# A two-layer decoder trunk: other orders in the embedding gate, at the layer boundary and in the last norm, and one more filler ahead of the gather

## The reference

```python
for i in range(2):
    x = x + mixer_block(rms_norm(x, ln_mix_g[i]), ...)            # projections, conv, attention, conv module
    x = x + hier_moe(rms_norm(x, ln_ffn_g[i]), ...)               # top-2 of 32 experts
    h = rms_norm(x, ln_ple_g[i])
    x = x + sigmoid(h @ w_ple_gate[i]) * (p[i] @ w_ple[i])        # the embedding gate
return rms_norm(x, final_norm_g)
```

## Time and profile before

| | before |
|---|---|
| time, median of 3 runs | 1158.5 us (1156.49 to 1158.56) |
| the profiled execution: time | 1154.8 us |
| the profiled execution: span from first to last instruction | 1153.0 us |
| PE busy | 95% of the span |
| DVE busy | 56% |
| ACT busy | 31% |
| mean granted TensorE clock | 0.989 of 2.4 GHz |

### The profile page before, as it was taken

The page is one execution under the profiler, slowest core; times in us unless marked ns, Lnnn a source line. Parts: engine busy times, 40 slices in busy tenths (PEclk is TensorE's granted clock), DMA queues, the critical chain, the costliest instruction groups (busy, mean ns, idle before and its releaser), DMA issues.

```text
span 1153.0 us, 21335 instructions
## 1 busy us (share of the span) xinstructions
PE 1091.3 (95%) x8152; PEld 858.7 (74%) x8152; DVE 650.3 (56%) x1353; ACT 354.4 (31%) x598; POOL 134.8 (12%) x163
## 2 busy tenths in 40 slices
PE   5999999999899999998899999999999999999985
PEld 5988998998755555554889799999886555555564
DVE  6687997545533333334768789964546333333365
ACT  4345442234321111112554454323333111111142
POOL 0121320110001001000002032101100100100000
PEclk9999999999999999999989999999999999999997
DMA  7557975555289999998454777555644999999951
GB/s 207 136 159 243 311 230 145 154 159 165 110 339 418 416 417 419 419 417 305 129 147 127 248 255 237 172 160 146 184 170 173 397 416 417 418 418 419 413 162 44
DMA packets 202981, 300.39 MB, mean 261 GB/s; under 512 B 14000, under 2 KB 166544, under 8 KB 186512
## 3 DMA queue, kind: packets, MB, share of 16 engines
q1 hardware_dynamic: 202896, 299.28, 73.3%
HBM read 298.21 MB, written 1.05 MB: 260 GB/s over the span
## 4 chain that ended last, share of the span: by engine, by line
PE 74%; DVE 12%; DMA 5%; issue 5%; ACT 2%; POOL 1%; SPq 1%; DVEq 0%; POOLq 0%; ACTq 0%
PE ps L729 72%; DMA gu_ring<-in_w_exp_up_dram 4%; DVE wsplit L1810 3%; PE ps L732 2%; DVE work L1932 1%; ACT wsplit L1276 1%; DVE work L1760 1%; DMA ring<-in_w_in_dram 1%; DMA ring<-in_w_o_dram 0%; DVE h_pair L2135 0%; DMA work<-in_x_dram 0%; DVE work L1880 0%; DVE work L1834 0%; DVE h_pair L1819 0%; DVE work L1904 0%
## 5 line engine op out<-in xcount | busy, mean ns | idle before, releaser
L729 PE MATMUL ps<-h_pair,wsplit 128*128 128x256 f32 x2880 | 369.8, 288 | 14.6 <-DVE h_pair L1819 7.4
L729 PEld LDWEIGHTS ps<-h_pair,wsplit 128*128 128x128 f32 x2880 | 356.1, 194 | 22.8 <-issue 14.8
L1810 DVE TENSOR_TENSOR wsplit<-ring,wsplit 128x1024 fp32r<-128x1024 f32 x136 | 167.4, 1235 | 71.7 <-ACT wsplit L1276 68.5
L1276 ACT ACTIVATE wsplit<-ring 128x1024 fp32r<-128x1024 f32 x136 | 141.6, 1055 | 198.2 <-PE ps L729 110.3
L729 PE MATMUL ps<-gu_ring,hT 128*64 128x256 f32 x896 | 107.6, 383 | 2.0 <-DMA gu_ring<-in_w_exp_up_dram 1.8
L1932 DVE SCALAR_TENSOR_TENSOR work<-work,convT 128x256 f32<-128x256 f32 x240 | 104.7, 508 | 0.0
L1503 ACT ACTIVATE prow<-ps 128x128 f32<-128x128 f32 x64 | 17.7, 277 | 277.0 <-PE ps L729 277.0
L2222 DVE TENSOR_TENSOR hT_r<-ps,hT_r 128x512 fp32r<-128x512 f32 x64 | 44.3, 692 | 93.6 <-ACT hT_r L1276 93.6
L729 PEld LDWEIGHTS ps<-gu_ring,hT 128*64 128x64 f32 x896 | 61.7, 137 | 46.6 <-issue 13.3
L2208 DVE TENSOR_TENSOR prow<-prow,ps 128x128 f32<-128x128 f32 x64 | 18.4, 288 | 131.6 <-ACT prow L1503 131.6
L729 PE MATMUL ps<-work,ring 128*128 128x256 f32 x384 | 85.7, 379 | 0.0
(11 more groups left out here) (211 smaller groups left out, 1139.5 us busy)
## 6 DMA issues: line engine op xcount, KB each, us to landing
ring<-in_w_in_dram SPq DMA_DIRECT2D x104, 512.0 KB, 4.7
down_ring<-in_w_exp_down_dram SPq DMA_DIRECT2D x40, 1024.0 KB, 19.1
gu_ring<-in_w_exp_gate_dram SPq DMA_DIRECT2D x28, 1024.0 KB, 14.7
gu_ring<-in_w_exp_up_dram SPq DMA_DIRECT2D x28, 1024.0 KB, 16.9
lent_down<-in_w_exp_down_dram SPq DMA_DIRECT2D x24, 1024.0 KB, 19.5
gu_last<-in_w_exp_gate_dram SPq DMA_DIRECT2D x12, 1024.0 KB, 13.9
gu_last<-in_w_exp_up_dram SPq DMA_DIRECT2D x12, 1024.0 KB, 16.1
ring<-in_w_exp_gate_dram SPq DMA_DIRECT2D x12, 1024.0 KB, 14.7
```

Of the source, the lines that this page charges most:

```text
L729: return nc.tensor.matmul(o, lhsT, rhs, start=first, stop=last)
L1276: return nc.scalar.activation(o, i, ACT.Copy)
L1810: TT(tile_split[:, m, 1, :, :], tile_of(name, m), tile_split[:, m, 0, :, :].bitcast(F32), ALU.subtract).then_inc(tile_low, 1)
```

## The change

It changes the order of instructions at four places, adds a filler in each layer, and computes the last norm in another way.

- `project_open`: the products of a kind are put together. First all of chunks 0 to 5 (high by high for both halves, then high by low for both, then low by high for both), then all three kinds of chunks 6 and 7 for m = 0, then for m = 1.
- `keep_busy` ahead of the gather runs 2 fillers instead of 1.
- `open_gate`: ACT squares all four pairs before it rounds the tiles of pg1. DVE makes two of the additions of squares ahead of the first low tile of pg1, and the others between the two.
- The gate and the boundary: ACT rounds the first tile of pg3 before the sigmoids and the second right after two of them; DVE takes pg2 before the first product, finishes three pairs of `xT`, splits all three, and takes pg3 only after that (in layer 1, which has no next layer, there is no split).
- The last norm: DVE multiplies the tokens in PSUM by the gain first, into the new `x_gain`, while the sum of squares is under way. PE's sum goes over four tiles (0 and 1, which hold pairs 0 to 2 added, and 6 and 7) instead of one, so two additions of squares are left out. The norm is then applied to `x_gain` by DVE for the first half of each row block and by ACT for the second.

```diff
@@ end of SP's program
-                    sp.wait_ge(pmul_ready[DEPTH], 2 * t + half + 1)
+                    sp.wait_ge(act_scaled if half else pmul_ready[DEPTH], t + 1)
@@ PE, project_open
-                    for chunks in (range(DC - 2), range(DC - 2, DC)):
-                        for m in range(2):
-                            rounded_rows(m, chunks)
-                        for m in range(2):
-                            rest_of_rows(m, chunks)
-                            rest_of_weights(m, chunks)
+                    early, late = range(DC - 2), range(DC - 2, DC)
+                    for m in range(2):
+                        rounded_rows(m, early)
+                    for m in range(2):
+                        rest_of_rows(m, early)
+                    for m in range(2):
+                        rest_of_weights(m, early)
+                    for m in range(2):
+                        rounded_rows(m, late)
+                        rest_of_rows(m, late)
+                        rest_of_weights(m, late)
@@ PE, ahead of the gather
-                keep_busy(UI["pp2"] % BANKS, 1)
+                keep_busy(UI["pp2"] % BANKS, 2)
@@ PE, end_of_all
-                    stat("mix", [sq_x[:, 0, :]], [(sq_added[l], all_added("mix"))])
+                    stat("mix", [sq_x[:, c, :] for c in (0, 1, 6, 7)], [(sq_added[l], 2), None, (sq_ready[l], 4), None])
@@ ACT, open_gate
-                    square_pair(0)
-                    square_pair(1)
-                    high_tile(l, "pg1", 0)
-                    square_pair(2)
-                    square_pair(3)
-                    high_tile(l, "pg1", 1)
+                    for i in range(4):
+                        square_pair(i)
+                    high_tiles(l, "pg1")
@@ ACT, gate and boundary
                 high_tiles(l, "pg2")
+                high_tile(l, "pg3", 0)
                 ple_sigmoid(0)
                 ple_sigmoid(1)
-                high_tile(l, "pg3", 0)
-                next_high(0)
                 high_tile(l, "pg3", 1)
                 ple_sigmoid(2)
-                next_high(1)
                 if l + 1 < DEPTH:
+                    next_high(0)
                     high_tile(l + 1, "kv", 0)
-                next_square(0)
-                next_high(2)
-                if l + 1 < DEPTH:
+                    next_high(1)
                     high_tile(l + 1, "kv", 1)
-                ple_sigmoid(3)
-                next_square(1)
-                next_square(2)
-                next_high(3)
-                next_square(3)
+                    next_high(2)
+                    ple_sigmoid(3)
+                    for i in range(3):
+                        next_square(i)
+                    next_high(3)
+                    next_square(3)
+                else:
+                    for i in range(2):
+                        act.wait_ge(x_gated, 4 * l + i + 1)
+                        next_square(i)
+                    ple_sigmoid(3)
+                    for i in (2, 3):
+                        act.wait_ge(x_gated, 4 * l + i + 1)
+                        next_square(i)
+
+            act.wait_ge(pow_ready[DEPTH], 1)
+            for t in range(TC):
+                act.wait_ge(gain_applied, TC + t + 1)
+                nc.scalar.activation(xout[:, t, 512:D], x_gain[:, t, 512:D], ACT.Copy, scale=col[:, 0, 1, t:t + 1]).then_inc(act_scaled, 1)
@@ DVE, open_gate
                     low_tile(l, "pg0", 1)
+                    add_square_pair(l, "ple", sq_p, 1)
+                    add_square_pair(l, "ple", sq_p, 2)
                     low_tile(l, "pg1", 0)
-                    add_squares("ple", sq_p, 4)
+                    add_square_pair(l, "ple", sq_p, 3)
+                    add_last_squares(l, "ple", sq_p, 4)
                     low_tile(l, "pg1", 1)
@@ DVE, gate and boundary
                 low_tile(l, "pg3", 0)
+                take("pg2", two(ple_t[2]))
                 ple_mul(0)
                 add_gated(0)
-                take("pg2", two(ple_t[2]))
                 low_tile(l, "pg3", 1)
                 ple_mul(1)
                 add_gated(1)
+                ple_mul(2)
+                add_gated(2)
+                dve.wait_ge(x_gated, 4 * l + 1)
                 if goes_on:
                     dve.wait_ge(vec_ready, 2 * (l + 1) + 2)
                     next_low(0)
-                ple_mul(2)
-                add_gated(2)
-                if goes_on:
                     next_low(1)
+                    next_low(2)
                     low_tile(l + 1, "kv", 0)
-                dve.wait_ge(x_gated, 4 * l + 1)
-                take("pg3", two(ple_t[0]))
-                if goes_on:
-                    next_low(2)
-                else:
-                    add_square_pair(l + 1, "mix", sq_x, 1)
-                    add_square_pair(l + 1, "mix", sq_x, 2)
-                ple_mul(3)
-                add_gated(3)
-                if goes_on:
+                    take("pg3", two(ple_t[0]))
                     low_tile(l + 1, "kv", 1)
+                    ple_mul(3)
+                    add_gated(3)
                     next_low(3)
                     add_square_pair(l + 1, "mix", sq_x, 1)
                 else:
-                    add_square_pair(l + 1, "mix", sq_x, 3)
-                    add_last_squares(l + 1, "mix", sq_x, 4)
+                    take("pg3", two(ple_t[0]))
+                    add_square_pair(l + 1, "mix", sq_x, 1)
+                    ple_mul(3)
+                    add_gated(3)
+                    add_square_pair(l + 1, "mix", sq_x, 2)
@@ DVE, last norm
+            dve.wait_ge(init_loaded, 48)
+            for half in range(2):
+                for t in range(TC):
+                    dve.wait_ge(tok_psum[l], 2 * half + 2)
+                    at = slice(half * 512, (half + 1) * 512)
+                    TT(x_gain[:, t, at], ps[:, 4 + 2 * t + half, :], gfull[:, at], ALU.mult).then_inc(gain_applied, 1)
             mean("mix", D)
             dve.wait_ge(pow_ready[l], 1)
-            dve.wait_ge(init_loaded, 48)
-            dve.wait_ge(tok_psum[l], 4)
+            dve.wait_ge(x_gated, 4 * DEPTH)
             for t in range(TC):
-                for half in range(2):
-                    STT(xout[:, t, half * 512:(half + 1) * 512], ps[:, 4 + 2 * t + half, :], col[:, 0, 1, t:t + 1],
-                        gfull[:, half * 512:(half + 1) * 512], ALU.mult, ALU.mult).then_inc(pmul_ready[l], 1)
+                dve.wait_ge(gain_applied, t + 1)
+                TS(xout[:, t, 0:512], x_gain[:, t, 0:512], col[:, 0, 1, t:t + 1], None, ALU.mult).then_inc(pmul_ready[l], 1)
```

More of the change, by code:

```diff
@@ L322, in program @@
         xout = area(9216, TC, D)
+        x_gain = area(0, TC, D)
         ang = area(8192, 4, S)
@@ L454, in program @@
         x_gated = sem("x_gated")
+        gain_applied = sem("gain_applied")
+        act_scaled = sem("act_scaled")
         psig_ready = sem("psig_ready")
@@ L1558, in next_high @@
                     act.wait_ge(x_gated, 4 * l + i + 1)
-                    if l + 1 < DEPTH:
-                        for c in (2 * i, 2 * i + 1):
-                            last = nc.scalar.activation(h_high[:, c, :], xT[:, c, :], ACT.Copy, scale=vcol("mix", c))
-                        last.then_inc(rows_high[l + 1], 1)
+                    for c in (2 * i, 2 * i + 1):
+                        last = nc.scalar.activation(h_high[:, c, :], xT[:, c, :], ACT.Copy, scale=vcol("mix", c))
+                    last.then_inc(rows_high[l + 1], 1)
                 def next_square(i):
```

## The result

| | kernel before | changed kernel |
|---|---|---|
| median (range), us | 1157.49 (1154.75 to 1158.56), 4 runs | 1143.07 (1141.55 to 1145.49), 4 runs |
| the profiled execution, us | 1154.8 | 1145.49 |
| its span, us | 1153.0 | 1143.7 |
| mean granted clock | 0.989 | 0.994 |

A forecast was written before the change was run, and what follows sets the result against it. PE was taken as busy 95% of the span, its gaps in the changed stretches set by ACT and DVE steps. Gains 0.65 + 0.45 + 2.9 + 1.4 + 3.85 = 9.25 us gave 1158.5 - 9.3 = 1149.2 us, range 1145.5 to 1153.7.

The forecast's parts named there:

- the term for the filler: Gather of layer 0: a second filler shortens the gap and keeps the clock up, 1.4 us; layer 1 counted 0.
- Openings: Where the gates open: PE no longer idles before the sum of squares; gain 0.65 us in layer 0, 0.45 in layer 1.
- The cover by pg0: Openings: ACT's four squares run while PE multiplies pg0; without that cover they would cost 1.1 us on the path.
- Boundary: Layer 0 to layer 1: earlier tiles and `xT` pairs bring 4.25 us, less 1.35 for a clock fall: 2.9 us.
- The charge for one fall of the clock: Boundary: new gaps bring one low stretch of about 3.3 us, 15 matmuls instead of 26, costing 1.35 us.
- 0.4 us as the worst: Gather of layer 1: the second filler counts 0, at worst a loss of 0.4 us, as the gap there is short.
- End, to the power: Last norm: POOL's power starts 4.3 us earlier, 0.45 of it from the opening, so the end's term is 3.85 us.
- The clock rival: Clock falls at gather (+1.4), boundary (+1.4) and last sum (+1.5) add 4.3 us: 1153.5 us; chance 0.20.
- the likeliest case: Whole kernel: the forecast itself, within 2.5 us of 1149.2 us, last sum taken at full clock; chance 0.62.
- The change doesn't do what it says: PE's work is the bound, expert loads absorb upstream gains, about half the end remains: 1156.5 to 1158.5 us; chance 0.07.
- slower: New boundary gaps keep TensorE at 1.2 GHz into layer 1; about 32 us low gives 1161 us; chance 0.04.
- The boundary gives nothing: Splits ahead of pg3's take put ACT and DVE in series, losing the boundary's 2.9 us: 1152.1 us; chance 0.07.

The follow-up runs named there:

- b1: Kernel before with only the new order in `open_gate`, both layers; ratio 1.0001, median 1155.95 us.
- c2: Changed kernel with one filler ahead of the gather instead of two; ratio 0.9930, median 1146.71 us.
- b3: Kernel before with only the second filler ahead of the gather added; ratio 1.0000, median 1155.83 us.
- b4: Kernel before with only the new gate order of layer 1 and the new last norm; ratio 0.9966, median 1151.58 us.
- e2: Changed kernel plus one filler in PE's wait for the last pair of `xT` at the boundary; ratio 0.9909, median 1144.46 us.
- d4: Changed kernel with the old last norm but the new gate order of layer 1; ratio 0.9918, median 1146.83 us.
- b2: Kernel before with only the new gate order of layer 0 and the new `project_open`; ratio 0.9982, median 1154.12 us.
- e4: Changed kernel with no filler ahead of the gather; ratio 0.9930, median 1146.03 us.
- c1: Changed kernel itself, run again in a second comparison with the kernel before; ratio 0.9929, median 1147.34 us.
- e1: Changed kernel itself, run a fourth time against the kernel before; ratio 0.9924, median 1146.57 us.
- c3: Changed kernel with the gate of layer 0 and `project_open` in the old order; ratio 0.9943, median 1148.01 us.
- d2: Changed kernel with PE's opening of layer 0 moved ahead of the end of the branch; ratio 0.9947, median 1149.73 us.

## Why the prediction was right or wrong

**Which step failed.** The forecast missed at the low end of its range, 1143.07 us for 1145.5 to 1153.7. The step that failed is the last of its sum, 1158.5 - 9.3 = 1149.2: it took the median of three runs for the time of the kernel before. The mean of 72 runs is 1155.7 us, so the base was 2.8 us too high. By the means of all runs the change gives 9.8 us (1155.7 to 1145.95 in 22 runs), so the gain was 0.5 us too small. The remaining 2.9 us are the spread of the four runs of the changed kernel, whose median lies that much under the mean of the 22. Within the gain the term for the filler was too large, the stores and PE's start behind the branch were put at nothing and measured 1.5 us won and 1.4 us lost, and these errors largely cancelled. Part by part:

**Openings: right.** No idle time before the sums, gains of 0.77 and 0.62 us to the sum for 0.65 and 0.45. The cover by pg0 held. In layer 0 PE starts later than before, so the stretch from its first matmul says less there; but from the filler to the sum b1 and c2, in which it starts early, take 12.12 us where before, b3 and b4 take 12.66 to 12.91.

**Boundary: mechanism right, size of the fall too large.** Without a fall the step gave 4.25 us, so 26.90 - 4.25 = 22.65; the profiles at full clock show 22.77. The charge for one fall of the clock was 1.35 us, and it cost 0.5 to 0.8 (23.23 to 23.59 against 22.77), although nearly as many matmuls ran slowly as I had put there. The 34 matmuls from 581.97 took 5.61 us, where e2 at full clock takes 1.45 + 3.10 = 4.55 for them. But e2 waits 0.34 us for ACT's tile between the two groups, and PE at the low clock reaches it when it is ready. From the start of the 34 to the sum the difference is 5.44 - 4.97 = 0.47 us. The term left that wait out. Against the old order the step is smaller, though: before had its own fall, of twice the length, and the old order takes 25.2 us at full clock. The order is worth 2.5 us; the other 1.2 of the 3.65 is the difference of two falls. Over all profiles the new order averages 23.4 us in 11 and the old one 25.7 in 5, falls counted in, so 2.3 us. The fall stayed in 9 of 11 executions. The Trainium skill ("TensorE: Matmul & The Clock Gate", section "HAM oscillation — how this bites in real kernels") describes a kernel whose clock falls behind each long wait for data. The trace differs in this: here the fall came behind four waits for ACT and DVE, the longest of 1.4 us.

**Filler: mechanism right, worth too large.** Its term, 1.4 us, was the difference between the gathers of two layers in one execution. That is what a fall costs (1.43 us in the rows), not how often it comes: it needed the share of executions in which the clock would fall within this gather, 2 of 5 with one filler. The mechanism held: in no profile with two fillers did the clock fall there. The "0.4 us as the worst" is seen as a begin 0.46 us late in either layer, but it doesn't reach the first expert. Measured: 0.0 us with 1.3 on either side (b3), and about 0.9 us by the rows and the counts.

**End, to the power: right in size, wrong in its cause.** 4.24 us for 3.85. The forecast had the last pair of `xT` 3.4 us earlier and gave 0.4 us to the new sum and the products ahead of the power. Measured are 4.19 us at the last pair and 0.05 behind it, and d4 shows the old norm as fast to the power. So two errors partly cancel. The products do end last, as forecast (1134.65 + 2.48 = 1137.13, then the power at 1137.27), so what the additions left out save is spent on the products. The sum of 16 records took 1.95 us for 1.84 at full clock. At 1.2 GHz it is the bound, as in e2:

```profile
1133.76 3.16 PE L732 MATMUL ps<-ones,work 128*128 128x1 f32 x16
...
1137.20 0.69 POOL L1625 TENSOR_TENSOR col<-col,mhalf 128x2 f32<-128x2 f32 x1 [17.04 <-DVE col L1796]
```

To the power that makes 16.30 us, 1.0 more. The clock rival had 1.5 for it, and it happened in 6 of 13 profiles with the new end (15.86 to 16.50 us), which the likeliest case left out.

**End, stores: wrong.** That "the stores move the same 1 MB, so I take no more from that" put 0 where 1.64 us came in the two profiles and 1.2 + 0.3 on average (power to first store 1.24 for 1.50). The step before the stores was read as hidden by them; it wasn't. The way from the power to the first store, for which the forecast changed nothing, became 0.26 us shorter.

**Losses: not seen.** 1.41 us for PE's later start behind the branch, which b2, which has one filler and nothing of the openings, shows too (4.25 us), as do all the variants with the full change but c2 (2.74). e4, still shorter by one filler, has 4.27. So neither a part nor a count of instructions sets it in an orderly way, and its cause stays open; that it goes with where the code lies in the program is a guess. It can cost more than the 1.4 us, as c1 shows, with the low clock for 3.4 us from 551.2 on:

```profile
550.41 7.48 PE L732 MATMUL ps<-p_pair,wsplit 128*128 128x256 f32 x48 [2.06 <-issue]
```

In the changed kernel's first profile the same 48 matmuls take 5.98 us. Of the 12 executions in which PE starts more than 4 us after the filler, 6 have such a fall in the opening, which makes it 1.5 us longer (10.67 for 9.18 to the sum); of the five in which it starts within 3 us, none has. Neither of the two profiles first compared has it, c1 and e1 do. And up to 1.2 us in the experts, which take 223.7 to 225.2 us in layer 0 in all the profiles, with no order by kernel. "Behind each of these places PE's list simply runs on" was true of the waits and not of what varies by itself.

**The time.** Term by term the sum was 9.25, the profiles differ by 9.3, and all comparisons together give 9.4; that they agree so well is luck. In the two profiles 3.2 us of losses that the sum didn't have (branch, experts, layer 1) stand against 3.2 us of gains that it put too low (stores 1.64, boundary 0.75, openings 0.46, to the power 0.39). The first comparison lay 4.4 us further, and 5.0 us from the mean of the other three. Single runs of the kernel before spread with a standard deviation of 1.9 us (72 runs, 1151.5 to 1160.2), those of the changed kernel with 2.3 (22 runs), so a difference of four against four has some 1.5 us, and 4.4 us is rare even so. About 1.6 of it goes with the clock: those four runs had a mean granted clock of 0.994 against 0.991 for all 22, and over the 22 runs each 0.0015, which is one low stretch of 3.4 us in the span, goes with 0.9 us (correlation -0.68; 0.6 us in the kernel before). The rest isn't explained; the comparisons ran on different chips, which nothing here separates from the spread. The range failed at its low end: it allowed 2 us for spread and the full clock together, though the base of 1158.5 was a median of three runs, which later lay 2.8 us above the mean of 72. The runs of before in the first comparison are the same executions again, the three shown and the profiled one, with a median 1.8 us above the mean of 72. With the 2.9 us by which the changed kernel's four lay low, that makes up the 4.7 us between 14.4, the difference of the two medians, and 9.8. The base's error and the spread of the new runs both belonged into the range, on both sides.

**Rivals.** "The change doesn't do what it says" and "slower" are out by every comparison. "The boundary gives nothing" is out by c3. The clock rival is half true: its falls come, each in some executions, in both kernels.

## What to carry to other kernels

Read what the clock does over several executions before a single fall is put into a sum: a fall in one profile is a price to be multiplied by how often it comes, and a filler that works against it can be worth less than the totals can tell. Orders that let TensorE run through gave here 2.5 us at the boundary and 4.2 us at the end. The first was worked out to 0.1 us from the starts of DVE's steps, the second to 0.4, with two errors that partly cancelled. For a kernel whose single runs spread by 2 us, the median of three is an error of the forecast like any other term.

## What was not expected of the hardware

- Apart from the one in which the program ends, each stretch at the low clock in these traces is 3.4 us long or twice that. Executions of one and the same kernel have them at different places: the changed kernel at 581 and 864 in one, at 271, 551, 585 and 868 in another. A profiled execution had from two to six, the one at the end counted.
- PE's start behind the end of a branch takes from 2.5 to 4.4 us after the last filler in layer 0, and 1.84 us in layer 1 in all executions, where no branch ends in between. Why is not shown. Moving work ahead of it moved the idle time (2.47 us in d2) behind that work.
- The expert stage of layer 0, whose code is the same in all these kernels, differs by up to 1.5 us between profiled executions, with TensorE at full clock in all of them.
